# A chunked gated delta scan: token turns, key products and weight-row dot products placed elsewhere in the loop

## The reference

```
Gcum  = cumsum(g)                                # within a chunk
decay = exp(Gcum_i - Gcum_j) for j <= i, else 0
A     = strictly lower part of (beta * k) @ k^T * decay
t_inv = inverse(A + I)
W     = t_inv @ (beta * k * exp(Gcum));  U = t_inv @ (beta * v)
attn  = (q @ k^T) * decay
for each chunk n:                                # the scan, S is 128 x 128
    v_new = U_n - W_n @ S
    o_n   = (q_n * exp(Gcum)) @ S + attn_n @ v_new
    S     = S * g_tot_n + (k_n * exp(Gcum_last - Gcum))^T @ v_new
```

## Time and profile before

| | |
|---|---|
| three runs | 1892.75, 1893.69, 1896.63 us; median 1893.69 |
| profiled execution | 1892.75 us, its span 1890.9 us |
| TensorE busy | 1800.7 us (95% of the span) |
| VectorE busy | 1247.4 us (66%) |
| ScalarE busy | 999.5 us (53%) |
| GpSimd busy | 146.9 us (8%) |
| chain that ended last | PE 85%, DVE 9%, ACT 3% |
| DMA | 283.29 MB, mean 150 GB/s |

### The profile page before, as it was taken

How to read it: one execution, slowest core, us unless ns; L and a number is a source line. 1 busy time by engine, 2 the same in 40 slices (tenths; PEclk the granted TensorE clock), 3 DMA queues, 4 the chain that set the end, 5 groups by cost and what they waited for, 6 DMA issues and landing times.

```text
span 1890.9 us, 34482 instructions
## 1 busy us (share of the span) xinstructions
PE 1800.7 (95%) x11798; PEld 1613.8 (85%) x11798; DVE 1247.4 (66%) x2520; ACT 999.5 (53%) x2003; POOL 146.9 (8%) x118
## 2 busy tenths in 40 slices
PE   8999999999999976899999999999899999999997
PEld 1877879998899966788999999999799888889997
DVE  2785447664399979766666666666766666348886
ACT  2545633341156678666555555555657656036665
POOL 0000003410184420000000000000000000000000
PEclk9999989999999999999999999999999999999999
DMA  7523223234455510355555555555354433445553
GB/s 264 193 100 101 89 67 102 79 120 135 136 185 173 175 56 1 103 196 190 189 189 189 184 187 184 189 188 188 122 202 155 149 116 108 155 167 178 187 181 120
DMA packets 77268, 283.29 MB, mean 150 GB/s; under 512 B 8576, under 2 KB 8576, under 8 KB 76928
## 3 DMA queue, kind: packets, MB, share of 16 engines
q1 hardware_dynamic: 77184, 282.16, 44.7%
HBM read 281.08 MB, written 1.05 MB: 149 GB/s over the span
## 4 chain that ended last, share of the span: by engine, by line
PE 85%; DVE 9%; ACT 3%; issue 1%; DMA 1%; POOL 1%; PEld 0%; PEldq 0%; ACTq 0%; POOLq 0%; SPq 0%; DVEq 0%
PE banks L831 19%; PE banks L819 17%; PE banks L893 8%; PE banks L429 7%; PE banks L1032 7%; PE banks L760 4%; PE banks L1044 3%; PE banks L612 2%; PE banks L593 2%; DVE split L2054 2%; PE banks L1005 1%; PE banks L783 1%; DVE arena L2052 1%; PE banks L400 1%; PE banks L601 1%
## 5 line engine op out<-in xcount | busy, mean ns | idle before, releaser
L1330 ACT ACTIVATE split<-arena 128x512 fp32r<-128x512 f32 x508 | 319.0, 629 | 145.3 <-PE banks L819 83.3
L819 PEld LDWEIGHTS banks<-split 128*128 128x128 f32 x3072 | 379.5, 192 | 11.1 <-DVE split L1991 3.1
L819 PE MATMUL banks<-split 128*128 128x256 f32 x3072 | 383.0, 283 | 3.2 <-DVE split L1991 2.3
L831 PE MATMUL banks<-split 128*128 128x512 f32 x1536 | 363.5, 390 | 2.7 <-issue 2.7
L2068 DVE TENSOR_TENSOR split<-arena,split 128x512 fp32r<-128x512 f32 x412 | 281.5, 689 | 115.8 <-ACT split L1330 110.2
L831 PEld LDWEIGHTS banks<-split 128*128 128x128 f32 x1536 | 283.3, 188 | 58.4 <-issue 2.9
L1311 ACT ACTIVATE split<-arena 128x512 fp32r<-128x512 f32 x264 | 164.7, 628 | 109.4 <-PE banks L1032 52.3
L893 PE MATMUL banks<-split 128*128 128x256 f32 x1344 | 169.5, 286 | 4.0 <-DVE split L2143 3.9
L893 PEld LDWEIGHTS banks<-split 128*128 128x128 f32 x1344 | 164.7, 193 | 7.6 <-issue 5.9
L429 PE MATMUL banks<-split 128*128 128x256 f32 (+2 forms) x936 | 150.6, 322 | 4.3 <-DVE split L1654 3.4
L429 PEld LDWEIGHTS banks<-split 128*128 128x128 f32 (+1 forms) x936 | 134.1, 196 | 21.8 <-issue 7.6
(11 more groups left out here) (379 smaller groups left out, 2365.9 us busy)
## 6 DMA issues: line engine op xcount, KB each, us to landing
arena<-wstream SPq DMA_DIRECT2D x525, 512.0 KB, 3.3
arena<-x_t SPq DMA_DIRECT2D x1, 2048.0 KB, 13.1
arena<-matsa SPq DMA_DIRECT2D x1, 1234.0 KB, 6.3
out_t<-arena SPq DMA_DIRECT2D x4, 256.0 KB, 2.1
arena<-mats SPq DMA_DIRECT2D x1, 576.0 KB, 8.0
arena<-crow SPq DMA_DIRECT2D x1, 512.0 KB, 7.0
arena<-rows SPq DMA_DIRECT2D x1, 512.0 KB, 5.5
arena<-mats SPq DMA_DIRECT2D x1, 449.0 KB, 3.6
```

Of the source, the lines that this page charges most:

```text
L819: mm = pe.matmul(ps[:, 4 + b, 0:S], w_parts[:, c, (2 * m + half) % 4, P * k:P * k + P], h_parts[:, e, 4 * half + k, :], start=(half == 0 a ...
L831: mm = pe.matmul(ps[:, 2 * tt + half, :], g_parts[:, e, j % 2, P * tt:P * tt + P], w_parts[:, c, (2 * m + half) % 4, :], start=(first and ...
L1330: act.activation(w_parts[:, 0, (2 * m + half) % 4, :], ring[:, peer_slot(m), 512 * half:512 * half + 512], ACT.Copy).then_inc(sem["w_hi"], 1)
```

## The change

Four things are placed elsewhere, on TensorE, ScalarE and VectorE. No operation is added or dropped.

1. The eight token turns. Before, turns 0 and 1 stood ahead of `in_tile(38)`, 2 and 3 behind it, 4 and 5 in level 2, 6 and 7 in level 4 of round 0. Now two stand in each of the levels 1 to 4 of round 0. They use PSUM banks 6 and 7 alone. With that the first level's `Z` transposes need no wait for `tok_ready` any more.
2. The key products of the next round stand behind the updates of level 2 instead of between products and updates of level 3.
3. Two mod tails stand between the first inverse and level 1.
4. The other mod tails are dealt out as one for each level, with two in levels 1 and 2 of round 0 and in levels 4 and 5 of round 3. The table before was (2, 1, 1, 1, 2, 3), (1, 0, 1, 0, 2, 2), (1, 1, 0, 0, 2, 2), (1, 1, 1, 1, 2, 2).

```diff
-            TOK_BANK = (2, 3, 2, 3, 6, 7, 6, 7)
             def tok_turn(i):
-                if i in (4, 5):
-                    pe.wait_ge(sem["a_raw"], i - 3)
-                if i >= 2:
+                if i < 2:
+                    pe.wait_ge(sem["a_raw"], i + 1)
+                else:
                     pe.wait_ge(sem["tok_ready"], i - 1)
-                    mm = pe.transpose(ps[:, TOK_BANK[i], ...
+                    mm = pe.transpose(ps[:, 6 + i % 2, ...
             def level_products(n, l, d):
-                if l == 1:
-                    if n:
-                        pe.wait_ge(sem["wu_ready"], step_at(n - 1, d))
-                    else:
-                        pe.wait_ge(sem["tok_ready"], 3 + d)
+                if l == 1 and n:
+                    pe.wait_ge(sem["wu_ready"], step_at(n - 1, d))
...
             key_products(0, 1)
-            tok_turn(0)
-            tok_turn(1)
             in_tile(38)
-            tok_turn(2)
-            tok_turn(3)
...
                     for d in range(2):
                         level_products(n, l, d)
-                    if n == 0 and l in (2, 4):
-                        tok_turn(2 + l)
-                        tok_turn(3 + l)
+                    if n == 0 and l < 5:
+                        tok_turn(2 * l - 2)
+                        tok_turn(2 * l - 1)
...
-                    if n < 3 and l == 3:
-                        for d in range(2):
-                            key_products(n + 1, d)
                     for d in range(2):
                         level_update(n, l, d)
                     if n < 3:
                         for d in range(2):
                             if l == 1:
                                 decay_rows(n + 1, d)
+                            if l == 2:
+                                key_products(n + 1, d)
```

ScalarE's `tok_move` calls move to the same places. VectorE:

```diff
             dve.sem_inc(sem["tiles_done"], 1)
-            TAILS = (...)
+            for q in range(2):
+                mod_tail(next(tails))
...
-                    for q in range(TAILS[n][l - 1]):
+                    for q in range(2 if (n, l) in ((0, 1), (0, 2), (3, 4), (3, 5)) else 1):
                         mod_tail(next(tails))
```

More of the change, by code:

```diff
@@ L549, in tok_turn @@
                 for h in range(4):
-                    mm = pe.transpose(ps[:, TOK_BANK[i], P * h:P * h + P], src[:, h, P * tt:P * tt + P], ident)
+                    mm = pe.transpose(ps[:, 6 + i % 2, P * h:P * h + P], src[:, h, P * tt:P * tt + P], ident)
                 mm.then_inc(sem["tok_turned"], 1)
@@ L1235, in tok_move @@
                 dst = (ktok if i in (0, 1, 4, 5) else vtok)[:, (2, 3, 2, 3, 0, 1, 0, 1)[i], :, :].rearrange("p a b -> p (a b)")
-                act.activation(dst, ps[:, (2, 3, 2, 3, 6, 7, 6, 7)[i], :], ACT.Copy).then_inc(sem["tok_ready"], 1)
+                act.activation(dst, ps[:, 6 + i % 2, :], ACT.Copy).then_inc(sem["tok_ready"], 1)
             act.wait_ge(sem["decay_sums"], 1)
@@ L1251, in _ @@
             act.activation(dec["eT"], dec["eT"], ACT.Exp).then_inc(sem["decay_ready"], 1)
-            tok_move(0)
-            tok_move(1)
             in_out(38)
-            tok_move(2)
-            tok_move(3)
             for d in range(2):
@@ L1267, in _ @@
                             sem["t_ready"], 1)
-                    if n == 0 and l in (2, 4):
-                        tok_move(2 + l)
-                        tok_move(3 + l)
+                    if n == 0 and l < 5:
+                        tok_move(2 * l - 2)
+                        tok_move(2 * l - 1)
                     for d in range(2):
@@ L1878, in _ @@
             dve.sem_inc(sem["tiles_done"], 1)
-            TAILS = ((2, 1, 1, 1, 2, 3), (1, 0, 1, 0, 2, 2), (1, 1, 0, 0, 2, 2), (1, 1, 1, 1, 2, 2))
+            for q in range(2):
+                mod_tail(next(tails))
             for n in range(4):
```

## The result

The changed kernel is slower: 1914.87 us, median of four runs (1913.41 to 1916.58), against 1895.16 before; the ratio is 1.0092, its 95% interval [1.0072, 1.0111]. The direction was forecast, the size was not: 17.4 us by the ratio (13.6 to 21.0 by its interval) instead of 11.8, and the median lies above the range of 1899 to 1911. The two medians of four are 19.7 us apart; over nineteen executions of the changed kernel the median is 1911.98 us. Two more executions, of 3598.53 and 4488.40 us at a mean clock of 1.00, belong to a slow state and are in none of these figures. The profiled execution took 1909.08 us, 16.3 more than the profiled one before.

The account below looks back on a forecast made before the run. The prediction took TensorE's own instructions as the bound (154.99 of 156 us busy in the loop); its terms 1.64 + 6.88 + 0.6 + 2.7 = 11.8 us put the kernel at 1905 us, range 1899 to 1911.

Parts of the forecast that it names:

- the fall: Rival: new waits in the stage lower TensorE's clock; three falls of 1.6 us give +4.8, 1910 us; chance 0.08.
- the one at 1360: Stretch with TensorE 0.59 of 4 us busy, after which the clock fell to a mean of 0.60 for 4 us.
- Turns of tokens: Round 0, levels 1 and 3: two pairs of transposes now lie on TensorE's path, costing 0.76 and 0.88, 1.64 us.
- Key products: Behind level-2 updates of rounds 0 to 2: TensorE stands waiting for VectorE's gaps, net 1.75, 2.47 and 2.66, 6.88 us.
- GpSimd beside the gaps: Round 0, level 2: GpSimd's token scaling may hold up VectorE's gap rows; 0.6 us, between 0 and about 1.25.
- Mod tails: Round 1 level 4, round 2 levels 3 and 4: tails delay the mask that updates await; 2.7 us (1.11 to 3.45).
- Sum at full clock: The four terms for the stage, 1.64 + 6.88 + 0.6 + 2.7, give 11.8 us; bounds 9.6 and 13.2.
- Nothing comes back behind the stage: Behind the stage nothing changes; the rest of the kernel was to keep equal length.
- TensorE's busy time: In the stage, a sign in the profile after: busy time unchanged, idle time up by 10 us.

Follow-up runs that it names:

- after_again: The changed kernel unaltered, run and traced once more beside the kernel before; median 1910.24 us, ratio 1.0094.
- tails_moved: The kernel before with only the mod tails dealt out anew, two of them ahead of level 1; median 1908.78 us, ratio 1.0089.
- turns_back: The changed kernel with the token turns placed as before; tails and key products stay moved; median 1915.97 us, ratio 1.0125.
- kp_filled: The changed kernel with 28 unread identity matmuls added where TensorE waited ahead of the moved key products; median 1911.42 us, ratio 1.0097.
- kp_moved: The kernel before with only the key products moved behind the level-2 updates; median 1906.26 us, ratio 1.0075.
- kp_back: The changed kernel with the key products in level 3 again; turns and tails stay changed; median 1902.90 us, ratio 1.0054.
- tails_back: The changed kernel with the mod tails placed as before; turns and key products stay moved; median 1908.43 us, ratio 1.0076.

## Why the prediction was right or wrong

**The step that failed** is the one that priced the waits at full clock. The prediction named the fall as a rival, gave it 4.8 us and the sum 16.6 with it, and then gave it a chance of 0.08, because no stretch of 4 us in the loop would be as empty as the one at 1360. The measured loop is 17.5 us longer, 12.9 of it at full clock and 4.6 more with the falls. That 4.8 came so near is in part luck: it stood for three falls, one in each wait for the gaps, and the changed kernel had two there, none in round 0, and one behind the 1.45 us wait for a mask. The reasoning set the new waits against a place where the clock held (2.79 of 4 us busy at 684) and one where it fell (0.59 of 4), and put them near the first. The runs put them on the other side: with the idle time filled, the loop goes from 174.53 to 169.97, 169.99 and 169.99 us. The Trainium skill's rule that idle gaps between groups of matmuls throttle the array ("TensorE: Matmul & The Clock Gate", section "HAM oscillation") was waved off by that comparison; the trace agrees with the rule here: 3.54 us from gap to level-3 products where the wait was idle, 2.68 where it was filled.

**Turns of tokens**, 1.64 us: 1.70 alone. Right. The release of the mask turn did not move either, as forecast: where the clock was full from the stage's first matmul on, the second mask turn began 9.20 us behind it before (262.78 to 271.98) and 9.19 in after_again (261.15 to 270.34). The changed kernel's 269.12 comes from a stage that began earlier, at 258.23. That they cover the two tails ahead of level 1 was right too: without them 1.31 and 2.27 us of waiting (tails_moved, turns_back). The 0.7 us given for the case without them was too small, since GpSimd's scaling beside the tails was not seen.

**Key products**, 6.88 us: the waits for the first gap are 1.58 and twice 2.04 us, 5.7 in all where the prediction looked for about 7, since the slower first group covers most of the wait for the second gap; but the inserted piece is larger. Round 0: updates end at 281.25 and level 3 begins at 285.15, 3.90 instead of 3.53; in kp_filled, at full clock, rounds 1 and 2 have 4.70 (321.59 to 326.29) and 4.71 instead of 4.45 and 4.44. A group that follows a wait takes 1.16 us instead of 0.89, as the one at 323.70 did before; this row was there and I used 0.89. With that the term is 2.12 + 2.72 + 2.93 = 7.8 us (rounds 1 and 2 with the added matmuls between the groups).

**GpSimd beside the gaps**, 0.6 (0 to 1.25): the lower half. VectorE's timeline of the changed kernel:

```profile
283.39 0.55 DVE L1794 TENSOR_SCALAR arena<-arena 128x512 f32<-128x512 f32 x1
283.86 2.06 DVE L1784 SCALAR_TENSOR_TENSOR arena<-arena 128x1024 f32<-128x1024 f32 x1
```

The first gap's TENSOR_SCALAR won the tie (0.43 us, and GpSimd's operation that began 0.07 us behind it took 1.25 instead of 1.04) and the second took 0.55 instead of 0.43: 0.1 us, and the second gap comes 2.69 us behind the updates instead of 2.59. What the trace of before could not show is shown: a TENSOR_SCALAR is held too, 0.54 to 0.55 us in all eight traces with the turns moved, 0.43 in the six without. In kp_moved, where GpSimd is elsewhere, the inserted piece of round 0 is 3.78 us instead of 3.90. That agrees with the Trainium skill ("SBUF — State Buffer", section "Who interferes with whom"); only its arrival, not the rule, decided the price. The tail behind it is the one that is hindered, 2.06 us, and there TensorE has other work.

**Mod tails**, 2.7 us (1.11 to 3.45): the updates of round 1, level 5 start 1.43 us later (forecast 1.0, bound 1.34), those of round 2, levels 4 and 5, 0.60 and 0.70 later (0.7 and 1.0), and each group of updates behind a wait takes 2.00 us instead of 1.85 or 1.73. Together 3.3. Nothing at level 2 and in round 3, as said.

**Sum at full clock**: 1.7 + 7.8 (GpSimd's 0.1 is in it) + 3.3 = 12.8, and 12.9 measured with the fillers in. 11.8 was forecast. The half clock adds 4.6 in the first trace of the changed kernel (174.53 - 169.97), which makes the 17.5 us of the loop and agrees with the 17.4 of the ratio. From execution to execution it varies: the nineteen of the changed kernel lie between 1908.39 us at a mean clock of 0.984 and 1917.76 at 0.980.

**Nothing comes back behind the stage**: from the loop's end to the last instruction 1463.6 us, against 1461.9 and 1462.9 in the two traces of before.

**TensorE's busy time** was to stay the same and its idle time to grow by 10 us. Idle grew by 8.4, and busy, by the clock above all, by 9.1.

Which waits let the clock fall can be narrowed. The fourteen profiled executions have twenty stretches at 1.2 GHz in the loop: three and four in the two of the changed kernel, two in kp_moved, two in kp_back, four each in tails_back and turns_back, one in tails_moved. Every one begins in a wait of TensorE for VectorE of 1.31 to 2.27 us or at most 2.1 us behind its end. All ten waits of 2.04 us have one; of the fifteen others in these bounds ten do. Behind the shorter waits, 0.16 to 1.27 us, none begins.

What stays open is why five of these waits have no fall behind them, and what sets how long a fall lasts. The wait of 1.45 us was followed by a fall in the changed kernel and kp_back and by none in kp_filled. Nor is a wait's length all: ahead of the loop TensorE waits 2.22 us for its first matmul in the stage, and in the first trace of before no fall follows, while in the second one begins in it.

## What to carry to other kernels

Where one engine's own instructions are the chain, price a new wait on TensorE twice: at its length, and with the work behind it at half clock; a forecast that kept the second only as a remote rival was too low here. Moving a producer earlier on a saturated engine gains nothing if its reader isn't waiting, and costs whatever its own input is late. And fill-in work on a side engine (the mod tails) costs nothing only in the levels where the saturated engine has other work between its product and its next use.

## What the runs showed of the hardware that I had not expected

- Waits of 2.04 us in a stage that was 99% busy before are enough for TensorE's clock to fall from 2.4 to 1.2 GHz (kp_moved, whose only waits over 0.6 us in the loop are 1.58, 2.04 and 2.04 us: a fall at both of 2.04 and none at 1.58, mean clock 0.97, loop 11.4 us longer; by the rounds above some 7.7 of it, an estimate, are waits and work at full clock).
- Fallen, it can stay low while TensorE is busy without a gap: 18.00 of 18 us busy at a mean clock of 0.53 in kp_back.
- Between 28 and 47 useless matmuls in the waits made the changed kernel's loop 4.6 us shorter in the profiled executions; only with 47 did the timing show a gain, and its five executions were more alike.
- The first group behind a wait takes 0.15 to 0.27 us longer (a group counted x8 or x16 in the timeline, with the clock at 1.00: 1.16 instead of 0.89, 2.00 instead of 1.85 or 1.73). I put it down to lost overlap, which no run isolates.
